# Gate scatters without add for heads 0 to 4, other heads' equal experts summed on VectorE, later choices spread over five blocks, loads moved

## The reference

```
v1, i1 = lax.top_k(s[..., 0, :], PEER_TOPK)         # 128 scores each, 16 kept
v2, i2 = lax.top_k(s[..., 1, :], PEER_TOPK)
cand = v1[..., :, None] + v2[..., None, :]          # 16 x 16
cv, ci = lax.top_k(cand.reshape(...), PEER_TOPK)
expert = e1 * N_KEYS + e2                           # e1, e2 taken from i1, i2 by ci
gate = jax.nn.softmax(cv, axis=-1)
pre = jnp.einsum('tkd,td->tk', expert_u[expert], xt)
act = jax.nn.gelu(pre, approximate=False) * gate    # k runs over all 8 heads x 16
out = jnp.einsum('tk,tkd->td', act, expert_v[expert])
```

## Time and profile before

| | us |
|---|---|
| median of 3 runs | 3912.24 |
| lowest, highest | 3906.52, 3913.24 |
| the profiled execution | 3917.48 |
| its span | 3915.9 |

### The profile page before, as it was taken

One profiled execution on the slowest core, in us unless ns is written; L12 is line 12 of the kernel. 1 busy time (PEld: TensorE's weight loads), 2 busy tenths in 40 slices (PEclk: granted clock), 3 DMA queues, 4 the chain that ended last, 5 costly groups with the idle time before them and its releaser, 6 DMA issues.

```text
span 3915.9 us, 55143 instructions
## 1 busy us (share of the span) xinstructions
PE 3655.3 (93%) x19324; PEld 3144.8 (80%) x19324; DVE 2659.9 (68%) x5202; ACT 1241.5 (32%) x1825; POOL 1943.8 (50%) x1352
## 2 busy tenths in 40 slices
PE   8989799998998999999999999999779999899998
PEld 6855498887876678899999999999558888787777
DVE  5443477775223348668887878877796666698887
ACT  3013343442112221333333333333233333333333
POOL 1023223231100118888888888888888888221120
PEclk9989899999999999999999999999899999999999
DMA  3249400002210135478888888887989998999997
GB/s 116 96 180 399 186 20 19 9 19 76 87 58 5 43 124 92 85 230 267 271 265 266 270 257 252 268 258 187 251 226 287 279 283 227 335 397 362 377 360 263
DMA packets 376223, 788.61 MB, mean 201 GB/s; under 512 B 136992, under 2 KB 245536, under 8 KB 342176
## 3 DMA queue, kind: packets, MB, share of 16 engines
q1 hardware_dynamic: 210208, 451.28, 34.2%
q0 software_dynamic: 165888, 336.01, 29.5%
HBM read 643.09 MB, written 144.05 MB: 201 GB/s over the span
## 4 chain that ended last, share of the span: by engine, by line
PE 25%; POOL 16%; DMA 7%; issue 6%; DVE 6%; DVEq 2%; ACT 1%; SPq 1%; POOLq 0%; ACTq 0%
POOL gates_d L2074 12%; PE peer_ps L2184 11%; PE peer_ps L2093 9%; PE peer_ps L2107 4%; DMA peer_gat<-gates_d 4%; DMA late_in<-gates_d 3%; POOL rows L2062 2%; POOL peer_rows L2062 2%; DVE late_rows L2467 1%; DVEq L2397 1%; DVEq L2481 1%; PE peer_ps L2130 1%; DVE peer_acc L2482 1%; DVE late_in L2489 1%; DVE peer_al L2501 1%
## 5 line engine op out<-in xcount | busy, mean ns | idle before, releaser
L2074 POOL DMA_INDIRECT gates_d<-peer_gates,peer_idx x768 | 1361.5, 1773 | 300.9 <-issue 220.9
L2093 PE MATMUL peer_ps<-high,peer_uh 128*128 128x384 f32 x2048 | 528.0, 338 | 39.3 <-DVE peer_ul L2384 33.4
L2093 PE MATMUL peer_ps<-low,peer_uh 128*128 128x384 f32 x2048 | 523.3, 336 | 0.0
L2093 PE MATMUL peer_ps<-high,peer_ul 128*128 128x384 f32 x2048 | 522.8, 336 | 0.0
L2093 PEld LDWEIGHTS peer_ps<-high,peer_uh 128*128 128x128 f32 x2048 | 369.3, 189 | 53.3 <-issue 46.3
L2184 PE MATMUL peer_ps<-peer_vh,peer_ah 128*128 128x512 f32 x1026 | 327.4, 401 | 52.8 <-DVE peer_al L2501 52.4
L2093 PEld LDWEIGHTS peer_ps<-low,peer_uh 128*128 128x128 f32 x2048 | 372.9, 189 | 0.0
L2093 PEld LDWEIGHTS peer_ps<-high,peer_ul 128*128 128x128 f32 x2048 | 372.7, 189 | 0.0
L2062 POOL DMA_INDIRECT late_rows<-in_expert_uv,peer_idx x108 | 135.4, 1253 | 416.5 <-DVE peer_acc L2482 367.4
L2184 PE MATMUL peer_ps<-peer_vh,peer_al 128*128 128x512 f32 x1026 | 320.0, 393 | 0.0
L2184 PE MATMUL peer_ps<-peer_vl,peer_ah 128*128 128x512 f32 x1026 | 318.9, 392 | 0.0
(11 more groups left out here) (478 smaller groups left out, 7588.4 us busy)
## 6 DMA issues: line engine op xcount, KB each, us to landing
late_in<-in_expert_uv SPq DMA_DIRECT2D x170, 512.0 KB, 5.5
gates_d<-mla_zeros POOLq DMA_DIRECT2D x128, 512.0 KB, 30.4
hidden_d<-peer_hid SPq DMA_DIRECT2D x128, 384.0 KB, 4.0
peer_raw<-in_expert_u SPq DMA_DIRECT2D x86, 512.0 KB, 5.1
peer_val<-in_expert_uv SPq DMA_DIRECT2D x86, 512.0 KB, 4.3
late_in<-hidden_d SPq DMA_DIRECT2D x170, 192.0 KB, 5.9
late_in<-gates_d SPq DMA_DIRECT2D x170, 192.0 KB, 6.9
first_raw<-in_expert_u SPq DMA_DIRECT2D x42, 512.0 KB
```

What stands on the lines that cost most here:

```text
L2074: pool.indirect_dma_start(gates_flat, bass.IndirectOffsetOnAxis(ap=idx[:, n, k:k + 1], axis=0), gates[:, n, k:k + 1], None, compute_op=ALU ...
L2093: last = nc.tensor.matmul(ps[i][:, a, 0:HD], w[:, cols], x[:, kc, a * HD:(a + 1) * HD], start=(kc == 0 and w is uh[i % 2] and x is high), ...
```

## The change

- `unit_pieces`: up to slot 14 as before, with a new piece 6 beside piece 5; in slots up to 143 the four steps are pieces 0 / 1, 2, 3 / 4 / 5, 6 instead of 0, 1 / 2, 3 / 4 / 5; from slot 144 on a unit takes six steps, of one piece each but for 5 and 6, so units begin five slots apart and end at slot 194.
- Scatters of heads 0 to 4 write (`bypass`) instead of adding. So that later writes hold the sum, dense units of heads 1 to 4 get piece 6: DVE compares their 16 experts with the 16 x head ones of the heads before (`prior_e`), multiplies by those heads' gates (`prior_g`), reduces and adds to its own. Heads 0 to 3 copy their gates to `prior_g`. `idx_ready` follows piece 6. Heads 5 to 7 still add.
- `rows_by`: the 148 early gathers are spread over dense units 7 to 32 instead of 7 to 29, the 28 over units 34 to 46 instead of 32 to 45.
- The output stage's inputs lie in other buffers (`val` is `raw`; `act_in` and `gat` have two of their own and the halves of `hid[0]`), `done` is `late_in`. So `load_out(0)` to `(2)` are issued after the stores of input blocks 124 to 126, and blocks 0 and 1 are split in the last two slots of the first pass.
- The two residual loads go from the start of the first output pass to behind the loads of blocks 24 and 80.

```
--- before.py
+++ after.py
@@ -1791,6 +1791,7 @@
 HOME_ROWS = 4
 WT = 2 * PH
 FIRST_UNIT = 3
+WRITTEN = 5
 
 
 def unit_order():
@@ -1806,7 +1807,12 @@
 
     at, slot = {}, FIRST_UNIT
     for n in range(UNITS):
-        steps = ((0, 1, 2, 3, 4), (5,)) if slot < WT - 1 else ((0, 1), (2, 3), (4,), (5,))
+        if slot < WT - 1:
+            steps = ((0, 1, 2, 3, 4), (5, 6))
+        elif slot < WT + NK:
+            steps = ((0,), (1, 2, 3), (4,), (5, 6))
+        else:
+            steps = ((0,), (1,), (2,), (3,), (4,), (5, 6))
         for i, pieces in enumerate(steps):
             at.setdefault(slot + i, []).extend((n, piece) for piece in pieces)
         slot += len(steps) - 1
@@ -1835,8 +1841,10 @@
         hid = [st.sb(f"hid{i}", [P, T]) for i in range(2)]
         ps = [st.psum(f"ps{i}", [P, 2, HALF]) for i in range(4)]
         sc, scw = [st.sb(f"sc{i}", [P, 2, NK]) for i in range(2)], st.sb("scw", [P, 2, NK])
-        cand, candw = st.sb("cand", [P, TOPK, TOPK]), st.sb("candw", [P, TOPK * TOPK])
-        sel = st.sb("sel", [P, 2, TOPK, TOPK])
+        work = st.sb("work", [P, 4 * TOPK * TOPK])
+        cand = work[:, 0:TOPK * TOPK].rearrange("p (a b) -> p a b", b=TOPK)
+        candw = work[:, TOPK * TOPK:2 * TOPK * TOPK]
+        sel = work[:, 2 * TOPK * TOPK:4 * TOPK * TOPK].rearrange("p (w a b) -> p w a b", w=2, b=TOPK)
         idx, gates = st.sb("idx", [P, UNITS, TOPK], U32), st.sb("gates", [P, UNITS, TOPK])
         identr = st.sb("identr", [P, P], F32R)
         pre = st.sb("pre", [P, SLOTS])
@@ -1851,9 +1859,11 @@
         with ExitStack() as home:
             early_rows = low_home["rows"] + [home.enter_context(nc.sbuf_tensor(f"peer_rows{i}", [P, 2 * D], F32))
                                              for i in range(HOME_ROWS, RING_IN)]
-        val = [st.sb("val", [P, D])] + [x[:, 0:D] for x in late_in]
-        act_in = [st.sb("act_in", [P, HALF])] + [x[:, D:D + HALF] for x in late_in]
-        gat = [st.sb("gat", [P, HALF])] + [x[:, D + HALF:2 * D] for x in late_in]
+            prior_e, prior_g = (home.enter_context(nc.sbuf_tensor(f"peer_{x}", [P, DENSE, WRITTEN - 1, TOPK], F32))
+                                for x in ("prior_e", "prior_g"))
+        val = raw
+        act_in = [st.sb(f"act_in{i}", [P, HALF]) for i in range(2)] + [hid[0][:, 0:HALF]]
+        gat = [st.sb(f"gat{i}", [P, HALF]) for i in range(2)] + [hid[0][:, HALF:T]]
         vh = [st.sb(f"vh{i}", [P, D], F32R) for i in range(2)] + [uh[0]]
         vl = [st.sb(f"vl{i}", [P, D], F32R) for i in range(2)] + [ul[0]]
         ah, al = ([st.sb(f"{x}{i}", [P, HALF], F32R) for i in range(RING)] for x in ("ah", "al"))
@@ -1890,7 +1900,7 @@
             "row_squared", "row_rooted", "row_inverted", "row_done"))
         block = st.block()
         gates_flat = gates_d.rearrange("j i t -> (j i t)").unsqueeze(1)
-        done = [raw[0], raw[1], hid[0], hid[1]]
+        done = [x[:, a * D:a * D + D] for x in late_in for a in range(2)]
         gain = rstd
         by_head = scores_d.rearrange("(h t) p w k -> h p w t k", h=PH)
         ss = ps[3][:, :, :].rearrange("p a (t k) -> p (a t) k", k=NK)
@@ -1911,7 +1921,12 @@
 
         def ahead(b):
 
-            return {WT + NK - 1: 0}.get(b)
+            return {OUT - 2: 0, OUT - 1: 1}.get(b)
+
+        def earlier_heads(n):
+
+            head, tile = units[n]
+            return tile < DENSE and 0 < head < WRITTEN
 
         def scatters(head, tile):
 
@@ -1944,9 +1959,9 @@
 
             if i < 7:
                 return 0
-            if i < 31:
-                return min(EARLY_SLOTS, EARLY_SLOTS * ((i - 7) * TOPK + k + 1) // (23 * TOPK))
-            return EARLY_SLOTS + (min(PASS_SLOTS, PASS_SLOTS * ((i - 32) * TOPK + k + 1) // (14 * TOPK)) if i > 31 else 0)
+            if i < 33:
+                return min(EARLY_SLOTS, EARLY_SLOTS * ((i - 7) * TOPK + k + 1) // (26 * TOPK))
+            return EARLY_SLOTS + (min(PASS_SLOTS, PASS_SLOTS * ((i - 34) * TOPK + k + 1) // (13 * TOPK)) if i > 33 else 0)
 
         @block.sync
         def _(sp):
@@ -1973,10 +1988,12 @@
                 tokens, n = slice(tiles[0] * P, tiles[-1] * P + P), len(tiles) * P
                 if q == 0:
                     sp.wait_ge(row_used, EARLY_SLOTS)
-                if q == 1:
-                    sp.wait_ge(mm_done, WT + NK)
-                if q >= 3:
+                if q < 3:
+                    sp.wait_ge(u_low, OUT + q - 2)
+                else:
                     sp.wait_ge(split_done, q - 2)
+                if q == 2:
+                    sp.wait_ge(stored[0], 16 * (NK // 2))
                 sp.dma_start(val[r][:, :], expert_uv[c * P:(c + 1) * P, D:2 * D]).then_inc(in_ready[r], 16)
                 if p == 0:
                     sp.wait_ge(stored[c % 2], 16 * (c // 2 + 1))
@@ -1985,6 +2002,13 @@
                     for tile in tiles:
                         sp.wait_ge(added[tile % 4], scatters(PH - 1, tile))
                 sp.dma_start(gat[r][:, 0:n], gates_d[c][:, tokens]).then_inc(in_ready[r], 16)
+
+            def load_rest(p):
+                tiles = PASSES[p]
+                sp.wait_ge(h_stored, 16)
+                sp.dma_start(rest[p][:, :, 0:len(tiles) * P],
+                             h_d[:, :, tiles[0] * P:tiles[-1] * P + P].rearrange("k p t -> p k t")
+                             ).then_inc(rest_ready[p], 16)
 
             def next_scores(slot):
                 for n, piece in pieces_of(slot):
@@ -2012,20 +2036,17 @@
                     load_raw(WT + c + 3)
                 sp.wait_ge(gelu_done, c + 5)
                 sp.dma_start(hidden_d[c][:, 0:TD], hid[c % 2][:, 0:TD]).then_inc(stored[c % 2], 16)
-                if c == NK - 3:
-                    load_out(0)
-            load_out(1)
+                if c >= NK - 4 and c < NK - 1:
+                    load_out(c - (NK - 4))
             next_scores(OUT)
-            for p, tiles in enumerate(PASSES):
-                sp.wait_ge(h_stored, 16)
-                sp.dma_start(rest[p][:, :, 0:len(tiles) * P],
-                             h_d[:, :, tiles[0] * P:tiles[-1] * P + P].rearrange("k p t -> p k t")
-                             ).then_inc(rest_ready[p], 16)
             sp.wait_ge(x_low, 2 * KC)
             sp.dma_start(gain[:, :], fin_row.broadcast_to([P, D])).then_inc(gain_ready, 16)
             for q in range(2, 2 * NK):
-                load_out(q)
+                if q > 2:
+                    load_out(q)
                 next_scores(OUT + q - 1)
+                if q in (24, NK - 48):
+                    load_rest(0 if q == 24 else 1)
                 if q == NK + 8:
                     for i, tile in enumerate(PASSES[0]):
                         sp.wait_ge(scaled_out, i + 1)
@@ -2072,7 +2093,9 @@
                     pool.wait_ge(added[tile % 4], scatters(head - 1, tile))
                 for k in range(TOPK):
                     pool.indirect_dma_start(gates_flat, bass.IndirectOffsetOnAxis(ap=idx[:, n, k:k + 1], axis=0),
-                                            gates[:, n, k:k + 1], None, compute_op=ALU.add).then_inc(added[tile % 4], 16)
+                                            gates[:, n, k:k + 1], None,
+                                            compute_op=ALU.bypass if head < WRITTEN else ALU.add
+                                            ).then_inc(added[tile % 4], 16)
                     for p in range(turn, rows_by(i, k)):
                         look_up(p)
                     turn = max(turn, rows_by(i, k))
@@ -2273,6 +2296,8 @@
             def highs_out(q):
                 act.wait_ge(in_ready[q % 3], 48 * (q // 3 + 1))
                 n = len(PASSES[q // NK]) * P
+                if q == 2:
+                    act.wait_ge(mm_done, OUT - 1)
                 if q >= RING:
                     taken(act, q - RING)
                 nc.scalar.activation(vh[q % RING][:, :], val[q % 3][:, :], ACT.Copy).then_inc(v_high, 1)
@@ -2349,7 +2374,8 @@
             for q in range(1, 2 * NK):
                 if q == NK + RING - 1:
                     halves()
-                highs_out(q)
+                if q > 1:
+                    highs_out(q)
                 row_gelu(OUT + q)
                 gates_exp(OUT + q)
                 if q == NK + 6:
@@ -2443,16 +2469,38 @@
                     dve.wait_ge(gate_exp, n + 1)
                     nc.vector.reciprocal(gsum[:, :], gsum[:, :])
                     dve.drain()
-                    tile = units[n][1]
-                    nc.vector.scalar_tensor_tensor(out=flat_e[:, :], in0=e12[:, 0, :], scalar=float(NK),
-                                                   in1=e12[:, 1, :], op0=ALU.mult, op1=ALU.add)
-                    nc.vector.tensor_scalar(gates[:, n, :], gexp[:, :], gsum[:, :], None, ALU.mult)
+                    head, tile = units[n]
+                    kept = tile < DENSE and head < WRITTEN - 1
+                    e = prior_e[:, tile, head, :] if kept else flat_e[:, :]
```

(34 more changed lines are left out.)

## The result

The changed kernel took 4109.45 us (median of 4 runs, 4065.74 to 4127.25) beside 3909.38 us for the kernel before: a ratio of 1.0474, 95% interval 1.0391 to 1.0557. The forecast was 3910 with 3950 as its upper end, so it failed, and by far more than any rival allowed. The profiled execution took 4114.35 us, its span is 4112.8.

A forecast was written before the change was run, and what follows sets the result against it. The prediction took POOL to be full in the first pass, making DVE late with rows, and DVE to have nearly no room. Terms 7 + 40 - 33 - 16 = -2 us gave 3910 us; range 3868 to 3950.

The forecast's parts named there:

- the first of the change's parts: POOL's scatters of heads 0 to 4 without add: mean 1.25 us busy, 0.5 us less each.
- (a): Query blocks, units 0 to 11: DVE's running sums make TensorE wait for `low`, +7 us.
- (b): First pass: DVE's sums and POOL's shortage of rows lose 88 us against 48 now, +40 us.
- the middle term: First pass, heads 5 to 7 still adding: POOL brings looked-up rows too slowly, 61 lost less 7 of lead, 54 us.
- (c): First output pass: five blocks per unit and earlier loads cut the 64 us lost to 31, -33 us.
- (d): Between the output passes: POOL's last scatter done earlier, so idle time and slow clock go, -16 us.
- (e): Second output pass: at its DMA limit, nothing changes, 0 us.
- Additions in waits: Rival, first pass: DVE's sums run where it waited for rows anyway; -33 us, 3879 us, chance 0.25.
- DVE's terms: First pass: losses from DVE's added running sums, 9 us early and 22 us late.
- Same price for both scatters: Rival, POOL: plain scatter costs as much as the add; about +46 us, 3958 us, chance 0.14.
- DVE outright the bound: Rival, queries and first pass: each new DVE step costs half as much again; +21 us, 3933 us, chance 0.15.

The follow-up runs named there:

- f: Kernel before with the scatters of heads 0 to 4 as plain writes, nothing else; 4045.4 us, ratio 1.0358.
- d: Changed kernel without the running sums, scatters of heads 0 to 4 still plain writes; 4134.31 us.
- c: Changed kernel with all scatters adding and without the running sums; 3940.33 us.
- g_pitch784: Changed kernel with gate rows of 784 floats instead of 1024, nothing else; 3883.45 us, ratio 0.9953.
- m: Kernel before with gate rows of 784 floats, nothing else; all scatters add; 3896.14 us, ratio 0.9995.
- k_pitch1008: Changed kernel with gate rows of 1008 floats instead of 1024; 3888.64 us, ratio 0.9974.
- b: Changed kernel with all scatters adding, the running sums kept; 3944.96 us, ratio 1.0101.
- g2: Changed kernel with 784-float gate rows and gathers over 23 and 14 units; 3828.98 us (0.9823), repeated in session 5 at 4060.66 us (1.0394).
- q: Changed kernel, heads 0 to 4 writing and summing only odd choices, even ones adding, gathers over 23 and 14 units; 3821.2 us, ratio 0.9799.
- j: Kernel before with only the choices' new places and the moved loads, all scatters adding, old gather spacing; 3900.2 us, ratio 0.9986.

## Why the prediction was wrong, point by point

**The step that failed** is the first of the change's parts: "No row shows an indirect write without one", whose cost I bounded from both sides, but only as time on POOL, from 1.57 us down to 1.00. I asked what the new instruction costs the engine that issues it, and put what it does to the engines that don't at nothing, without a reason. On POOL it is even cheaper than my lower end: 0.96 us (from 1450 to 1697 us the minimum is 952 ns and the median 958). Elsewhere it costs 145 us (f), 194 (d against c) or, from the same program in two sessions, 1.0394 against 0.9823, some 220 us. No rival covered this, since all three moved time between POOL and DVE. Where a change puts in an operation that no row shows, the range should have had an end for side effects on the others; mine had 40 us above the forecast.

**The rest of the sum held in the main.** g_pitch784 is the changed kernel in a session without starving (with a row length that is worth nothing in m, where all scatters add): 3883.45 beside 3903.72, so -20 where I forecast -2; k_pitch1008 gives -12.5. By steps:

(a) Query blocks, +7: b against c gives 7.2; in g the first input block starts 5.2 later than before.

(b) First pass, +40: in g it is 36.2 us longer than in the profiled execution of before (1168.6 against 1132.4). By pieces, each the time between the starts of its first and last block less 8.26 us a block: the blocks from 16 to 48 lose 10.7 us (forecast 9), those from 48 to 88 lose 59 (forecast 54), and those from 88 to 120 lose 24 (forecast 22). The last figure alone proves little, as the kernel before loses 24.4 us there too, without any sums. But g2, where the middle term is undone by the spacing of 23 units and DVE hardly waits for rows, keeps the outer two, 10.3 and 22.5, and q, with half of the sums, loses 1.9 and 13.0. What I took for a cost of the change as a whole was the cost of one number in it, 26 instead of 23.

(c) First output pass, -33: against 4.08 us a block its first 50 blocks lose 29.3 us in g and had lost 68.5, so -39; I had 64 and 31. In the changed kernel itself the first ten blocks lose 46.2, of which all but the 4.1 of g come with the starving, and the next 40 lose 23.1.

(d) Between the passes, -16: the ten blocks around the change of pass lose 10.8 us instead of 25.6, so -15, in the changed kernel as in g.

(e) Second pass, 0: behind those ten blocks the kernel before loses 27.9 us in its profiled execution, m 3.0 and g 4.1, though the medians of the first two don't differ; the other profiles lie between. I take that for the spread of an execution and no part of the change; nothing here shows where it comes from. Against m's profile the steps of g are +7, +44, -39, -19 and +1, together -6. That this lies so near to -2 is in part luck: (b) is 4 above the forecast, (c) 6 below.

**The rivals.** Additions in waits: partly true; where rows are short (b against c) the sums of the first pass are free, but in g and g2 DVE's terms show as forecast. Same price for both scatters: false, 0.96 against 1.57 us; but the arithmetic I made for it, 1097 us for 26 units against 998, so 99 later, is what c against j shows with every add kept (1216.7 against 1125.1 us, 92 more). The total I gave this rival was added wrongly: 99, 7, -33 and -15 make +58, or 3970, and not +46 and 3958. Kernel b makes its condition true and lies 44.8 us above the kernel before, which is near the wrong total by luck. DVE outright the bound: false. By the rule of the Trainium skill (SBUF — State Buffer, Who interferes with whom) I let DVE's two-input operations stretch POOL's bars. That went further than the section, which names GpSimd instructions that read SBUF and says of a probe that `tensor_tensor` did not stall a DMA. The trace agrees with the latter: the plain scatters' median of 958 ns beside a minimum of 952, in the stretch where the sums run, shows no such stretching here.

The other rule, that the bar of a DMA issued from GpSimd ends with the last descriptor written (the Trainium skill, Perfetto Trace Analysis, Per-instruction lifecycle), I read as "so the add is free on POOL". The trace: the bar fell by 0.61 us when the add went, and with it the packets from 128 to 16. So the add isn't free on POOL, and my reading was wrong. The rule itself isn't contradicted: if fewer packets mean fewer descriptors to write, a shorter bar is what it asks for. The trace shows packets only, so that step is argued.

**What stays open.** Which resource is short isn't shown. Three engines stop and go on in steps of 0.70 us without a semaphore, after some ten plain writes, while the DMA engines are at a share of 0.22. Instructions that arrive late would look like that, but the transfers of instructions, which the page has as queues of their own, don't bear it out. The kernel after:

```profile
q8 instruction: 35, 0.57, 0.1%
q14 instruction: 94, 0.77, 0.1%
```

The kernel before has 35 and 92 of these packets, at the same shares. From 1450 to 1697 us the trace has 15 of 8 KB and more, which took 10.8 us in all, against 19 and 15.6 us before; TensorE stops 48 times. If it is instructions that come late, the delay lies behind these transfers. The packets of the writes aren't held up either: the 512 of the first burst took at most 15 ns each and keep POOL's pace.

What makes a place starve isn't known. Sessions 1, 4 and 5 and the first one did, 2 and 3 did not; sessions 2 and 5 bear the same chip number in the records, so it may not be the chip alone. And whether the changed kernel at 1024 floats would run unstarved where g did was not tried.

## What to carry to other kernels

An operation that is cheaper on its own engine can be dear everywhere else: price a new kind of DMA by what the other engines do while many of it follow each other, and give the range an end for it. When several engines show short idle times "issue" side by side and nothing is busy, look for the engine that issues without pause, count how many of its instructions go by before the first stop, and break the row before that number: with the gathers back at their old spacing, half of the writes took 2.0% off, and all of them cost 3.9% in session 5. And before believing that an edit has cured a stall, repeat the sick kernel beside it in the same session; here three healthy runs stood for a cure, and the same program starved in the next session but one.

## What the runs showed of the hardware

- An indirect scatter of 128 single floats takes POOL 1.57 us and 128 packets with add (kernel before), 0.96 us and 16 packets without (kernel after).
- Plain ones every 1.26 us, 16 or 32 in a row, stop TensorE, its loader and DVE (TensorE for 0.2 to 3.1 us at a time), in some sessions and not in others: 134.5 to 157.1 us of TensorE's and its loader's time added up between 1450 and 1700 us, or 1.4. In the 35 bursts of the seven profiles that starve the first stop comes when 9 to 13 writes have begun, and the stops of different engines end 0.70 us or a multiple of it apart (for 51 of the loader's 52 stops in the kernel after). With every second one an add it was 1.4 and 11.0 us, with at most four under way 1.4 us, and 4.1 us in a session where the full dose starves.
- In the starved stretch TensorE's mean granted clock was 0.83 instead of 0.99 (the lower of its two levels, 1.2 GHz, for part of it), after idle times like those above, so that the stops cost more than their length: TensorE did 812 matmuls in 181.4 busy us instead of 1280 in 239.9, 4.5 per us instead of 5.3.
